# Another order of the softmax steps on VectorE, ScalarE and TensorE in an encoder's attention

## What is computed

```python
for i in range(DEPTH):                      # 2 layers
    h = rmsnorm(x, ln_mix[i])
    qkv = h @ w_qkv[i]
    q = rmsnorm(qkv[..., :nq].reshape(B, S, N_HEADS, HEAD_DIM), q_norm[i])
    k = rmsnorm(qkv[..., nq:nq + nk].reshape(B, S, N_KV_HEADS, HEAD_DIM), k_norm[i])
    v = qkv[..., nq + nk:].reshape(B, S, N_KV_HEADS, HEAD_DIM)
    if i % N_MIXERS == 0:
        o = global_attention(apply_axial_rope(q, ...), apply_axial_rope(k, ...), v)
    else:
        o = window_attention(q, k, v, rel_bias, sinks[i // N_MIXERS])
    x = x + o @ w_o[i]
    x = x + hier_moe(rmsnorm(x, ln_ffn[i]), w_group[i], w_expert[i], w1[i], w3[i], w2[i])
```

## Time and profile before

| | us |
|---|---|
| median of 3 runs | 658.33 (656.89 to 658.52) |
| the profiled execution | 658.52 |
| its span, first to last instruction | 656.6 |

### The profile page before, as it was taken

How to read it: one execution, slowest core, us unless ns; L and a number is a source line. 1 busy time by engine, 2 the same in 40 slices (tenths; PEclk the granted TensorE clock), 3 DMA queues, 4 the chain that set the end, 5 groups by cost and what they waited for, 6 DMA issues and landing times.

```text
span 656.6 us, 7951 instructions
## 1 busy us (share of the span) xinstructions
PE 633.7 (97%) x2959; PEld 281.9 (43%) x2959; DVE 205.8 (31%) x615; ACT 174.1 (27%) x422; POOL 71.4 (11%) x85
## 2 busy tenths in 40 slices
PE   8999899999999999999999999999999999999995
PEld 6445545733433433433344455465343343344331
DVE  1655533512302212221143666234212212113112
ACT  2126642212112113022141566321202202112112
POOL 0006550000000000000010578100000000000000
PEclk9999999999999999999999999999999999999998
DMA  9999806689999999999999995585999999999992
GB/s 326 284 292 421 308 1 266 246 326 421 422 422 414 420 372 423 422 421 423 405 314 238 386 402 173 194 354 217 423 420 421 416 422 371 425 421 423 421 423 89
DMA packets 43170, 229.61 MB, mean 350 GB/s; under 512 B 8239, under 2 KB 8529, under 8 KB 18562
## 3 DMA queue, kind: packets, MB, share of 16 engines
q1 hardware_dynamic: 41500, 224.66, 87.3%
q0 software_dynamic: 1312, 4.23, 2.0%
q10 hardware_dynamic: 326, 0.31, 0.1%
HBM read 228.10 MB, written 1.08 MB: 349 GB/s over the span
## 4 chain that ended last, share of the span: by engine, by line
PE 88%; DVE 4%; ACT 3%; issue 2%; POOL 2%; DMA 1%; DVEq 0%; ACTq 0%
PE ps L1334 34%; PE ps L1361 17%; PE ps L1112 11%; PE ps L1194 8%; PE ps L1295 4%; PE ps L1311 4%; PE ps L1147 2%; PE ps L1176 2%; PE ps L1163 1%; POOL attw L416 1%; ACT attw L533 1%; PE ps L1343 1%; PE ps L1259 1%; DMA ring<-in_ln_mix_dram 1%; PE ps L1056 1%
## 5 line engine op out<-in xcount | busy, mean ns | idle before, releaser
L1334 PE MATMUL ps<-ring,work 128*64 128x512 f32 x512 | 111.3, 592 | 0.0
L1334 PE MATMUL ps<-attw,work 128*64 128x512 f32 x512 | 111.2, 592 | 0.0
L1112 PE MATMUL ps<-attw,work 128*128 128x512 f32 x192 | 88.7, 605 | 0.0
L1361 PE MATMUL ps<-ring,work 128*64 128x512 f32 x384 | 85.9, 594 | 1.1
L944 DVE COPY work<-ps 32x512 f32<-32x512 f32 x64 | 43.7, 683 | 105.6 <-PE ps L1361 105.2
L933 DVE TENSOR_TENSOR work<-work,ps 128x512 f32<-128x512 f32 x16 | 11.0, 687 | 185.7 <-PE ps L1334 185.7
L1334 PEld LDWEIGHTS ps<-attw,work 128*64 128x64 f32 x512 | 36.8, 137 | 73.1 <-issue 73.1
L1334 PEld LDWEIGHTS ps<-ring,work 128*64 128x64 f32 x512 | 36.6, 137 | 72.2 <-issue 71.9
L605 ACT COPY work<-ps 32x512 f32<-32x512 f32 x64 | 36.9, 576 | 106.8 <-PE ps L1361 106.4
L416 POOL TENSOR_SCALAR attw<-attw,stat 128x256 f32<-128x256 f32 x64 | 59.0, 933 | 41.1 <-DVE stat L824 40.7
L1194 PE MATMUL ps<-attw,work 128*128 128x512 f32 x128 | 59.7, 601 | 2.8 <-issue 2.5
(11 more groups left out here) (152 smaller groups left out, 487.1 us busy)
## 6 DMA issues: line engine op xcount, KB each, us to landing
ring<-in_w_dram SPq DMA_DIRECT2D x112, 1024.0 KB, 16.2
attw<-in_w_dram SPq DMA_DIRECT2D x80, 1024.0 KB, 16.7
attw<-in_w_qkv_dram SPq DMA_DIRECT2D x4, 2048.0 KB, 20.8
attw<-in_w_o_dram SPq DMA_DIRECT2D x8, 1024.0 KB, 23.0
attw<-in_w_qkv_dram SPq DMA_DIRECT2D x4, 1024.0 KB, 13.5
ring<-bias_rows POOLq DMA_DIRECT2D x16, 256.0 KB, 7.1
x_sb<-in_x_dram SPq DMA_DIRECT2D x2, 512.0 KB, 5.8
out_dram<-x_sb SPq DMA_DIRECT2D x4, 256.0 KB, 2.7
```

What stands on the lines that cost most here:

```text
L1112: last = pe.matmul(ps[:, g, :], xT[:, k, P * tt:P * tt + P], wqkv[part][:, k, :], start=(k == 0), stop=(k == KB - 1))
L1334: last = pe.matmul(ps[64 * e:64 * e + 64, 6 + which, :], xg[:, k, c:c + 2 * SLOTS], w13(which, k // 4)[:, e, k % 4, :], start=(k == 0), st ...
L1361: last = pe.matmul(ps[64 * e:64 * e + 64, half, :], hT[:, k, 64 * e:64 * e + 64], w2(kh)[:, e, k % 2, 512 * half:512 * half + 512], start= ...
```

## The change

Only orders change, in three engines, in both layers alike.

- DVE: instead of two maxima and then two inversions per slice, the inversion of duo u-1 follows the maximum of duo u. The parts of `head_norm` for groups 4 and 5 are put one to a duo (u = 2 to 5 and 8 to 11), each behind the inversion. `copy_o` stands behind the maximum and inversion at u = 7, 11 and 15.
- ACT: `square_heads(4)` moves ahead of `exps(2)`. From u = 3 on `exps(u)` stands ahead of `copy_probs(u - 2)`. The Ln and Exp of group 4 follow `exps(3)`, those of group 5 `exps(9)`. `copy_q(2)` stands behind `copy_probs(3)`, `copy_q(3)` behind `copy_probs(9)`.
- PE: `turn_q(2)` moves from v = 2 to v = 1, and both late `turn_q` now follow `turn_probs(2v+1)` instead of preceding it.

```diff
@@ ACT @@
                 exps(1)
+                square_heads(4)
                 exps(2)
-                square_heads(4)
                 copy_probs(0)
-                exps(3)
-                copy_probs(1)
-                inverse_head_rms(4)
-                for u in range(4, DUOS):
-                    if u in (7, 11):
-                        copy_q((u + 1) // 4)
-                    copy_probs(u - 2)
+                for u in range(3, DUOS):
                     exps(u)
+                    if u == 3:
+                        inverse_head_rms(4)
                     if u == 7:
                         square_heads(5)
+                    if u == 9:
                         inverse_head_rms(5)
+                    copy_probs(u - 2)
+                    if u == 5:
+                        copy_q(2)
+                    if u == 11:
+                        copy_q(3)
@@ DVE @@
-                for v in range(SLICES):
-                    duo_max(L, 2 * v)
-                    duo_max(L, 2 * v + 1)
-                    if v == 1:
-                        head_norm(L, 4, 0)
-                    invert_sum(L, 2 * v)
-                    if v in (2, 4):
-                        head_norm(L, 3 + v // 2, 1)
-                    invert_sum(L, 2 * v + 1)
-                    if v in (2, 4):
-                        head_norm(L, 3 + v // 2, 2)
-                    if v == 3:
-                        head_norm(L, 4, 3)
-                        head_norm(L, 5, 0)
-                    if v == 5:
-                        head_norm(L, 5, 3)
-                    if v % 2 == 1 and v >= 3:
-                        copy_o(L, v // 2 - 1)
+                duo_max(L, 0)
+                for u in range(1, DUOS):
+                    duo_max(L, u)
+                    invert_sum(L, u - 1)
+                    if 2 <= u < 6:
+                        head_norm(L, 4, u - 2)
+                    if 8 <= u < 12:
+                        head_norm(L, 5, u - 8)
+                    if u % 4 == 3 and u >= 7:
+                        copy_o(L, u // 4 - 1)
+                invert_sum(L, DUOS - 1)
@@ PE @@
-                    if v in (2, 4):
-                        turn_q(1 + v // 2)
                     turn_probs(2 * v + 1)
+                    if v == 1:
+                        turn_q(2)
+                    if v == 4:
+                        turn_q(3)
```

## The result

The changed kernel takes 665.64 us (median of 4 runs, 664.54 to 666.12) against 658.37 us for the kernel before in the same comparison (4 runs, 656.89 to 658.52). The ratio is 1.0105 with a 95% interval of 1.0085 to 1.0126, so it is 1.05% or 7.3 us slower. The profiled execution took 665.68 with a span of 663.9, against 658.52 and 656.6 before: 7.3 us as well, so the two traces can be compared place by place. In this part L-numbers of the changed kernel are higher by 2 on DVE (the maximum is L811, the inversion L822 and L826, the copy of o L833) and lower by 5 in PE's attention (`turn_probs` L1158, `turn_q` L1127, `scores` L1142, `weigh` L1171, `project` L1189).

A forecast was written before the change was run, and what follows sets the result against it. PE, busy 97% of a 656.6 us span, was taken as the bound. Span 656.6 + 0.3 (layer 0) + 5.8 (layer 1) + 1.9 around it, less 0.2 for the median, gave 664.4 us; range 661.0 to 667.0.

The forecast's parts named there:

- the mechanism over DVE and POOL: Odd duos' reciprocals stand behind the next maximum, sometimes a copy of o; POOL's scaling and PE come 1.5 to 2 late.
- T(3): PE's turning of duo 3's probabilities; in layer 1 forecast at 381.2 where it was 379.31, +1.9 us.
- T(7): PE's turning of duo 7's probabilities; layer 1 at 395.15 instead of 392.70, +2.45; layer 0 at 73.8, -0.2.
- T(9): PE's turning of duo 9's probabilities; layer 1 at 401.6, its chain behind inverse norms that wait for ACT.
- scores(6): PE's scores of duo 6, waiting for copied q; layer 1 at 403.95 instead of 399.29, +4.7; layer 0 +0.2.
- T(11): PE's turning of duo 11's probabilities; layer 1 at 410.35 instead of 403.63, +6.7; layer 0 at 86.0, +1.5.
- T(15): PE's turning of duo 15's probabilities, last per layer; layer 1 at 420.35, +5.8; layer 0 at 95.25, +0.3.
- five stalls of 0.4: Upper bound of layer 1: each of its five stalls runs 0.4 longer, which the prediction gave as +7.5.
- Equal: Rival: layer 1's chain catches up as layer 0's does, each layer ends near +0.3, about 659 us; chance 0.12.
- Faster: Rival: waits for copied q, the copy of o and partly POOL go, about 654 us; chance 0.05.
- The clock falls: Rival: longer idle times put PE at 1.2 GHz over a piece of 6 to 7 us, about 671 us; chance 0.03.
- The rule on the shared ports: Two-input DVE steps and POOL exclude each other; moved norms beside two scalings could cost about 0.9 more each, about 666.2.

The follow-up runs named there:

- the control: The changed kernel measured once more, unaltered, in a later comparison: 664.85 us, 7.2 over the kernel before.
- ACT's and PE's order alone: Only ACT and PE get the change's new order, DVE keeps that of the kernel before: 665.43 us, 7.9 over before.
- the reciprocal alone: The changed kernel with the reciprocals of duos 7, 11 and 15 ahead of the copies of o: 662.36 us, 4.9 over before.
- both ways free: The changed kernel with reciprocals of duos 7, 11, 15 ahead of the copies of o, and copy_probs(6), copy_probs(10) ahead of exps(8), exps(12): 661.50 us, 3.9 over before.
- four parts undone: Changed kernel, urgent reciprocals ahead of o copies, copy_probs(6), (10) ahead of exps(8), (12), turn_q(3) and its copy earlier, group 4's norms later: 656.22 us, 1.0 under before.
- DVE's order alone: Only DVE gets the change's new order, ACT and PE keep that of the kernel before: 665.84 us, 8.4 over before.

## Why the prediction was right, and where it was not

The sign and the size held, and so did the mechanism over DVE and POOL: 664.4 forecast, 665.64 measured, +6.1 against +7.3. But the sum is nearer than its terms are, and that is luck in part. In the profiled execution layer 0 was under-priced by 1.3, the clock, which I had left out of the sum, added 1.4, layer 1 was over-priced by 0.8, and the stretches outside the attentions were 0.7 shorter; together that makes the 1.2 that were missed.

**Layer 1, place by place.** T(0) came 1.28 later than before in this execution (373.22 against 371.94, from the start-up and layer 0). With that taken off, the forecast's places and the measured ones are:

| place | forecast | measured less 1.28 |
|---|---|---|
| T(2) | 377.2 | 377.18 |
| T(3) | 381.2 | 380.95 |
| T(7) | 395.15 | 394.90 |
| T(9) | 401.6 | 401.07 |
| scores(6) | 403.95 | 403.36 |
| T(11) | 410.35 | 411.03 |
| T(15) | 420.35 | 420.97 |

Up to scores(6) the forecast runs up to 0.6 late, in small parts, one of which is that the four steps of the inverse norms took 0.88 (377.80 to 378.68) and not 1.0. Behind it the measured kernel is late by the half clock. Without that, in the control, scores(0) to T(15) takes 5.0 more than before where I forecast 5.8. So the layer's term was too high by 0.8 as the kernel runs at full clock. The signs that I named for this layer came: POOL's waits 7.1 ("about 8"), the four longest before T(3), T(7), T(9) and T(11), though at 1.1 to 1.6 us and not 1.5 to 2; one wait over 1 us before scores(6), 1.19; "issue" 0.3 before project(0). The norms waited for ACT behind E(3) and E(9), 1.33 each time, and DVE reached M(4) at 378.68, which is 377.40 less the 1.28. One sign failed: layer 0's stretch was to grow by less than 1, and grew by 1.6.

One bound was added up wrongly: five stalls of 0.4 on top of +5.8 are +7.8 and not +7.5, so the upper end of the range should have read 667.3.

**Layer 0 was mis-sized:** +0.3 forecast, with +1.2 as its bound, and +1.6 measured. From scores(0) on, T(3) was 1.25 later than before, T(7) 0.5, scores(6) 1.3, T(11) 2.85 and T(15) 1.6; forecast for the last four were -0.2, +0.2, +1.5 and +0.3. What I had said is given back, 0.7 each before T(12) and T(14), was given back (0.65 and 0.7). Two terms were missing or too small. At the start PE waited before T(2) for ACT's copy of T(1), and before T(3) for a longer scaling, and of that 0.9 was still left at T(6); T(7) then came 0.7 later than forecast, counted from scores(0). And scores(6) lost 0.5 more at its copy (the wait was 0.82 and not 0.33). Read as a place in the span T(7) looks right, 73.98 against 73.8, but that is luck: the attention of the changed kernel began 0.47 earlier. PE's rows of layer 0, T(2), T(3), scores(6) and T(11):

```profile
57.80 0.63 PE L1158 MATMUL ps<-consts,attw 128*128 128x128 f32 x4 [0.57 <-ACT attw L545]
...
60.63 0.66 PE L1158 MATMUL ps<-consts,attw 128*128 128x128 f32 x4 [0.48 <-POOL attw L416]
...
81.01 1.14 PE L1142 MATMUL ps<-attw 64*128 64x256 f32 x8 [0.82 <-ACT attw L522]
...
86.82 0.65 PE L1158 MATMUL ps<-consts,attw 128*128 128x128 f32 x4 [1.36 <-POOL attw L416]
```

**What I had overlooked** is ACT's way. The prediction moved `copy_probs(2v)` behind `exps(2v+2)` and never asked who waits for that copy. It made no error in the sum, because over DVE and POOL T(7) and T(11) were as late anyway; but the explanation was half of the truth, and the expectation for ACT's and PE's order alone, 2 to 4 us, missed the 7.9 for that reason. The expectations for the reciprocal alone and for both ways free were too hopeful as well.

**The rivals.** "Equal" fell: it held that lateness is caught up as in layer 0, and layer 0 itself didn't. "Faster" fell, although parts of it came true: the long wait before project(0) is gone in both layers, and with four parts undone the rest is no slower than before. "The clock falls" got 0.03 and came in part: not a piece of 6 to 7 us but three instruction groups, and 1.4 us instead of 6.5, in some executions.

**The rule on the shared ports.** POOL's scaling of duo 3 in layer 0 began at 58.39, while DVE's add of two SBUF inputs (L754) ran until the next instruction began at 58.80:

```profile
58.21 0.67 DVE L754 TENSOR_TENSOR attw<-work 128x512 f32<-128x512 f32 x1
58.80 0.68 DVE L800 TENSOR_REDUCE stat<-ps 128x2 f32<-128x512 f32 x1
...
59.88 0.26 DVE L759 TENSOR_TENSOR stat<-stat 128x8 f32<-128x8 f32 x1
```

```profile
58.39 3.99 POOL L416 TENSOR_SCALAR attw<-attw,stat 128x256 f32<-128x256 f32 x4 [0.79 <-DVE stat L826]
```

Two scalings took 3.99 here, and 3.63 where no such add runs beside them: 0.36 longer, about the 0.41 of the add that was left. The step at 59.88 ran beside the same scalings, with two inputs too, and took 0.26, not 0.9. In layer 1 the four steps of the moved norms took 0.88 beside S(2) and 0.96 beside S(8), the two-input steps among them 0.17 to 0.25 each. The Trainium skill, page "SBUF — State Buffer", section "Who interferes with whom", lets whoever is second wait for the whole instruction of the first. The trace agrees where POOL was second, and doesn't where DVE's small step was; the 666.2 that I had worked out by it from two blocks of 0.9 had no such blocks behind it. The prediction had the right result from a weak row: the norms at 379.40 ran for the most part beside the issue of a bias load (379.21 to 379.96), and only their end beside a scaling, which began at 380.01.

## What to carry to other kernels

In an order written by hand, write down for each step not only what it needs but what stands ahead of it in its engine's stream, and what those need: here a wait for PE's own result (4.29 us on an engine 31% busy) had got in front of what PE wanted next, and by a second way, over ACT, as well. When one cause is taken away and the time moves less than its waits did, look for a second way to the same instruction before giving up the theory. Interleaving may be right with few exceptions: four pieces put back turned +7.2 us into -1.0, but keeping the pairs and moving only what PE waited for gave -3.7.

## What the runs showed of the hardware that I had not expected

- The granted clock fell to the 1.2 GHz level for a stretch of layer 1's attention in four of the twelve profiles (the changed kernel, DVE's order alone, ACT's and PE's alone, both ways free), and not in the other eight, among them the changed kernel again. Ahead of a fall PE had stood idle two to five times in the layer's attention for about 1 to 1.9 us, never longer; with the same idle times it also stayed up in the changed kernel again. With DVE's order alone it fell at another place (columns as in the earlier trace rows):

```profile
384.00:386.00 2.00, 2.00 (x12) 0.77 (x8) 1.29 (x7) 1.03 (x5) 1.89 (x3) 0.51 1.01 418
```

- A POOL scaling that begins while DVE adds two SBUF tensors takes 0.36 us longer (2.18 against 1.82 in the kernel before, 3.99 against 3.63 for two in the changed one, twice in each profile's layer 0).
